# Latent attention with the keys on partitions, 512 queries moving, and the projections made head by head

## What is computed

```python
def mla_queries(c_q, q_norm_g, w_uq, rope):
    q = (rms_norm(c_q, q_norm_g) @ w_uq).reshape(B, L, MLA_HEADS, MLA_QK)
    q_nope, q_rope = q[..., :MLA_NOPE], q[..., MLA_NOPE:]
    if rope is not None:
        q_rope = apply_axial_rope(q_rope, *rope)
    return jnp.concatenate([q_nope, q_rope], axis=-1) * MLA_QK ** -0.5
...
    def one_block(qi):
        s = jnp.einsum('bqhd,bkhd->bhqk', qi, k, preferred_element_type=jnp.float32)
        p = jax.nn.softmax(s, axis=-1).astype(v.dtype)
        return jnp.einsum('bhqk,bkhd->bqhd', p, v)
...
    att = block_softmax_attention(q_lat, jnp.concatenate([k_lat, k_ctx], axis=1),
                                  jnp.concatenate([v_lat, v_ctx], axis=1))
```

## Time and profile before

| | |
|---|---|
| median of 3 runs | 4261.07 us (4256.55 to 4267.57) |
| span of the profiled execution | 4261.7 us |
| attention block, first layer | 440.3 us (503.1 to 943.4) |
| attention block, second layer | 391.8 us (2745.4 to 3137.2) |
| busy over the span: TensorE, VectorE, ScalarE, GpSimd | 87%, 53%, 33%, 31% |
| mean granted TensorE clock | 0.914 |

### The profile page before, as it was taken

How to read it: one execution, slowest core, us unless ns; L and a number is a source line. 1 busy time by engine, 2 the same in 40 slices (tenths; PEclk the granted TensorE clock), 3 DMA queues, 4 the chain that set the end, 5 groups by cost and what they waited for, 6 DMA issues and landing times. The chain is left out here.

```text
span 4261.7 us, 54579 instructions
## 1 busy us (share of the span) xinstructions
PE 3720.1 (87%) x20116; PEld 3116.5 (73%) x20116; DVE 2267.7 (53%) x3970; ACT 1415.5 (33%) x2841; POOL 1306.3 (31%) x1182
## 2 busy tenths in 40 slices
PE   6997688877847899999999897698968788999998
PEld 4897577766625688888888697577847767888886
DVE  4853566656663344444444752576766625445454
ACT  3112466651111422222223312466741123222222
POOL 1211011123331155555554211011123313545454
PEclk8998799997868899999999898799978899999999
DMA  5530000012013111111110630000040122111111
GB/s 188 192 110 3 28 1 13 1 54 112 20 43 141 50 40 39 39 39 39 34 35 10 203 121 4 25 1 11 6 157 20 45 95 69 59 39 52 47 49 54
DMA packets 145678, 243.97 MB, mean 57 GB/s; under 512 B 9480, under 2 KB 113689, under 8 KB 141915
## 3 DMA queue, kind: packets, MB, share of 16 engines
q1 hardware_dynamic: 138108, 208.57, 14.8%
q0 software_dynamic: 7392, 33.03, 2.1%
HBM read 215.60 MB, written 25.99 MB: 57 GB/s over the span
## 5 line engine op out<-in xcount | busy, mean ns | idle before, releaser
L2242 POOL TENSOR_TENSOR x<-x,mlp_tmp 128x512 f32<-128x512 f32 x576 | 785.5, 1396 | 805.9 <-DVE mlp_tmp L2223 800.8
L2223 DVE TENSOR_TENSOR mlp_tmp<-psum,gate 128x512 f32<-128x512 f32 x576 | 391.8, 689 | 273.2 <-POOL x L2242 194.6
L143 PE MATMUL psum<-act_hi,w_hi 128*128 128x512 f32 (+1 forms) x1280 | 472.8, 369 | 12.6 <-DVE w_lo L2201 12.6
L144 PE MATMUL psum<-act_lo,w_hi 128*128 128x512 f32 (+1 forms) x1280 | 472.5, 369 | 0.0
L145 PE MATMUL psum<-act_hi,w_lo 128*128 128x512 f32 (+1 forms) x1280 | 472.4, 369 | 0.0
L143 PE MATMUL psum<-w_hi,hidden_hi 128*128 128x512 f32 x1152 | 449.9, 391 | 0.0
L144 PE MATMUL psum<-w_lo,hidden_hi 128*128 128x512 f32 x1152 | 448.4, 389 | 0.0
L145 PE MATMUL psum<-w_hi,hidden_lo 128*128 128x512 f32 x1152 | 448.2, 389 | 0.0
L2215 DVE TENSOR_TENSOR hidden_lo<-square,hidden_hi 128x512 fp32r<-128x512 f32 x160 | 102.4, 640 | 592.6 <-ACT hidden_hi L2187 592.6
L1378 DVE TENSOR_REDUCE att_max<-psum 128x1 f32<-128x512 f32 (+2 forms) x272 | 217.9, 801 | 183.5 <-PE psum L145 183.3
L2179 ACT ACTIVATE relu<-psum 128x512 f32<-128x512 f32 x160 | 88.9, 555 | 666.8 <-PE psum L145 666.8
(11 more groups left out here) (325 smaller groups left out, 8608.3 us busy)
## 6 DMA issues: line engine op xcount, KB each, us to landing
w_raw<-in_mlp_w SPq DMA_DIRECT2D x128, 512.0 KB, 3.8
side_w<-in_w_ada SPq DMA_DIRECT2D x40, 1024.0 KB, 6.5
hy_tab<-in_hy_tab POOLq DMA_DIRECT2D x24, 1024.0 KB, 13.6
w_raw<-in_w_in SPq DMA_DIRECT2D x32, 512.0 KB, 4.6
ada_w<-in_w_ada SPq DMA_DIRECT2D x8, 1024.0 KB, 11.5
x<-in_x SPq DMA_DIRECT2D x4, 2048.0 KB, 14.6
wo_raw<-in_w_out SPq DMA_DIRECT2D x16, 512.0 KB, 5.6
hy_scratch<-hy_out POOLq DMA_DIRECT2D x24, 256.0 KB, 3.1
```

The costliest lines, as they stand in the source:

```text
L143: pe.matmul(out, lhs[0], rhs[0], start=start, stop=False)
L144: pe.matmul(out, lhs[0], rhs[1], start=False, stop=False)
L2223: dve.tensor_tensor(tmp[:, j % 2, :], ps[:, 4 + j % 4, :], gate[:, int(t >= LAT_TILES), 512 * h:512 * h + 512], ALU.mult).then_inc(gated.s ...
L2242: pool.tensor_tensor(a, a, tmp[:, j % 2, :], ALU.add).then_inc(added.sem, 1)
```

## The change

The attention block is written anew; nothing outside it changes but two tables and the column order of two weights, which are arranged before the launch.

Scores are made with keys on partitions and 512 queries moving (`score`), so the probabilities come out in the layout that the product with the values needs and are not turned. The softmax maximum of a query is then no longer a value per partition. It is found beforehand from a one-pass product of the high parts with queries on partitions (`rough_scores`, a `max_ctx` and four `max_lat` for each block of 512 queries), reduced by VectorE, turned into a row by four transposes (`max_row`), and written with its sign changed by ScalarE into one spare row of the query tile; the key tile holds ones in that row, so the score product itself subtracts it.

The work goes in blocks of one head and 512 queries, and a block in five slots of two key tiles each (in the first layer a block of one slot for each pair of heads holds the context queries). ScalarE takes two exponentials of each slot, one rounded to fp32r into `ph` and one in full precision; VectorE subtracts the two in slots 0, 2 and 4 of a block, GpSimd in slots 1 and 3 (`on_pool`). The value product (`weigh`) runs two slots later in three passes of 512 columns; its weights hold 64 columns of ones beside the 64 values, so it also gives the row sums, which VectorE inverts in two pieces of 64x256 (`invert`) and multiplies in (`normalize`).

Projections are made head by head, channels on partitions, between the slots: the side tasks `q`, `k`, `v` and the maxima of the next block are dealt out over the half slots and share PSUM banks 0 and 1. The rotation of the queries takes two products on VectorE and four instructions on GpSimd for each 512 columns. Both layers' first tasks (`opening`) run before the first slot. At the start of the block GpSimd clears and fills the constant rows, and TensorE and ScalarE wait for it (`fixed`).

```diff
 def latent_first_loads(kit, l, sp):
 
-    QW, KVW = HG * MLA_QK, HG * (MLA_NOPE + MLA_V)
...
+    sp.dma_start(ukv_raw[:], kit.io["mla_w_ukv"][l]).then_inc(kit.sig("lat_ukv_raw", 16).sem, 16)
+    sp.dma_start(uq_raw[:], kit.io["mla_w_uq"][l].rearrange("(t p) n -> p t n", p=P)).then_inc(kit.sig("lat_uq_raw", 16).sem, 16)
+    sp.dma_start(rope[:], kit.io["rope"]).then_inc(rope_in.sem, 16)
+    sp.dma_start(rope_t[:], kit.io["rope_t"]).then_inc(rope_in.sem, 16)
...
+    on_pool = {s for s, (b, j) in enumerate(slots) if j in (1, 3)}
+
+    def max_tasks(b):
+        if blocks[b].context:
+            return [("max_ctx", b, 0), ("row", b, 0)]
+        return [("max_ctx", b, 0)] + [("max_lat", b, i) for i in range(4)] + [("row", b, 0)]
+
+    opening = [("v", 0, g) for g in range(3)] + [("kr", 0, g) for g in range(3)]
+    opening += [("k", 0, g) for g in range(3)] + [("q", 0, g) for g in groups] + max_tasks(0)
+    side = {}
+    for b, block in enumerate(blocks):
+        todo = []
+        if not block.context:
+            todo = [t for n in (b + 1, b + 2) if n < len(blocks) and (n == b + 1 or blocks[n - 1].context) for t in max_tasks(n)]
+            h, p = block.heads[0], block.heads[0] // 2
+            if block.col0 == 0 and h + 1 < MLA_H:
+                todo += [("q", h + 1, g) for g in groups]
+            at = 2 * (h % 2) + (block.col0 > 0)
+            if p + 1 < MLA_H // 2:
+                todo += [("k", p + 1, at)] if at < 3 else []
+                todo += [("v", p + 1, g) for g in {1: [0], 3: [1, 2]}.get(at, [])]
+        n = 2 * block.slots
+        for i in range(n):
+            side[(first[b] + i // 2, i % 2)] = todo[i * len(todo) // n:(i + 1) * len(todo) // n]
...
+            def score(s):
+                b, j = slots[s]
+                if j == 0:
+                    pe.wait_ge(rowed.sem, rowed[b])
+                if s >= 2:
+                    if s - 2 in on_pool:
+                        pe.wait_ge(exped.sem, exped[s - 2])
+                    else:
+                        pe.wait_ge(lo_dve.sem, lo_dve[s - 2])
+                for i in range(2):
+                    k0 = blocks[b].key_tiles[2 * j + i] * P
+                    for h, cols, at in blocks[b].parts():
+                        last = three_pass(pe, ps[:, S0 + 2 * (s % 2) + i, at],
+                                          [a[h // 2 % 2][h % 2][:, k0:k0 + P] for a in (keys_h, keys_l)],
+                                          [a[h % 2][:, cols] for a in (query_h, query_l)], True, True)
...
+            for s in range(n_slots + 2):
+                if s < n_slots:
+                    score(s)
+                    for t in side[(s, 0)]:
+                        side_task(t)
+                if s >= 2:
+                    weigh(s - 2)
+                if s < n_slots:
+                    for t in side[(s, 1)]:
+                        side_task(t)
...
+                scores = ps[:, S0 + 2 * (s % 2):S0 + 2 * (s % 2) + 2, :]
+                act.activation(ph[s % 3][:], scores, ACT.Exp, scale=SCALE)
...
+                    act.activation(scores, scores, ACT.Exp, scale=SCALE).then_inc(exped.sem, 1)
...
+            for b in range(2):
+                for e in range(2):
+                    link(pool, pool.memset(keys_h[b][e][SWAP[e], :].bitcast(F32), 1.0))
+                    link(pool, pool.memset(keys_l[b][e][SWAP[e], :].bitcast(F32), 0.0))
+            for e in range(2):
+                link(pool, pool.memset(query_h[e][SWAP[e], :].bitcast(F32), 0.0))
+                link(pool, pool.memset(query_l[e][SWAP[e], :].bitcast(F32), 0.0))
+            for b in range(2):
+                link(pool, pool.memset(v[b][:, :, V_ONES, :].bitcast(F32), 1.0))
+                link(pool, pool.memset(v[b][:, :, V_ZEROS, :].bitcast(F32), 0.0))
+            pool.memset(kr2[:, :, 32:64], 0.0).then_inc(fixed.sem, 1)
...
+                link(pool, clear)
+                link(pool, pool.tensor_tensor(rot[rows, :], rot[rows, :], rot2[rows, :], ALU.add))
+                link(pool, pool.tensor_copy(query_h[h % 2][rows, cols], rot[rows, :]))
+                pool.tensor_tensor(query_l[h % 2][rows, cols], rot[rows, :], query_h[h % 2][rows, cols].bitcast(F32),
+                                   ALU.subtract).then_inc(roped.sem, 1)
+                pool.wait_ge(roped.sem, roped[t])
...
+            for s in range(n_slots):
+                for t in side[(s, 0)]:
+                    side_task(t)
+                if s in on_pool:
+                    pool.wait_ge(exped.sem, exped[s])
+                    pool.tensor_tensor(pl[s % 3][:], p_sb[:], ph[s % 3][:].bitcast(F32), ALU.subtract).then_inc(lo_pool.sem, 1)
...
+                    if g < 2:
+                        turns = [q for q in tasks[:tasks.index(t)] if q[0] == "q" and q[2] < 2]
+                        if turns:
+                            dve.wait_ge(roped.sem, roped[turns[-1]])
+                        dve.tensor_tensor(rot[ROPE[e], :], bank(t)[ROPE[e], :], rope_t[ROPE[e], cols], ALU.mult)
+                        dve.tensor_tensor(rot2[ROPE[e], :], bank(t)[SWAP[e], :], rope_t[SWAP[e], cols], ALU.mult)
...
+                        link(dve, dve.reciprocal(den[NUM[h % 2], b % 2, c], den[NUM[h % 2], b % 2, c]))
...
+            for s in range(n_slots + 3):
+                if s < n_slots:
+                    for i in range(2):
+                        for t in side[(s, i)]:
+                            side_task(t)
+                    if s not in on_pool:
+                        probs_low(s)
+                if s - 2 in final:
+                    invert(final[s - 2], 0)
+                if s - 3 in final:
+                    invert(final[s - 3], 1)
+                    normalize(final[s - 3])
```

721 lines of the change are left out of this document (371 added, 350 removed).

## The result

The changed kernel took 4411.3 us (4406.7 to 4430.3), the kernel before 4259.1 beside it: ratio 1.0359, 95% interval 1.0336 to 1.0383. The forecast was 4360 in a range of 4215 to 4430, so direction and range held; the likeliest case's own range, 4320 to 4400, ended 11 us short. Of the priced cases the measurement lies between the likeliest, 4363, and the slower clock, 4440, and nearer the second.

A forecast was written before the change was run, and what follows sets the result against it. TensorE's streamed columns bound the attention before; after, its work shrinks but openings, queue stalls and ends add 54.9 us in the second layer and 46.8 in the first: +101.7 on 4261.7 gives 4363, rounded to 4360, range 4215 to 4430.

The forecast's parts named there:

- the likeliest case: Whole kernel: TensorE's work plus opening, queue stalls and end, with nothing absorbed; 4363 us, chance 0.45.
- the slower clock: Rival: TensorE's clock falls in 31 waits of near 3 us, adding 80 us; 4440 us, chance 0.13.
- TensorE's work: Attention by head: 40.8 us after against 45.4 before in the second layer, 43.5 after in the first.
- the sum: Both attention blocks: 446.7 us in the second layer and 487.1 in the first, together +101.7 us.
- The rival by work alone: Queues absorb the stalls and TensorE is the bound throughout; 4219 us, faster, chance 0.20.
- The opening: Start of each layer's attention block to the first slot: 58 us, 58.5 in the first layer, with 11 of TensorE work.
- The gate: Block start: TensorE waits for `fixed` behind 17 GpSimd memsets, so the first product starts 20 us into the block.
- The wait at the row: Before the row transposes TensorE waits for the last maximum: 2.8 us in block (h, 512), 1.1 in (h, 0).
- the rotation: Query rotation: GpSimd's chain takes 4.1 us; one `rot` buffer makes VectorE's second `q` wait, 2.9 us per head.
- The row that the forecast set against this rival: Evidence against the slower clock: before the change, gaps of 1 us left the clock at 0.97.
- The reciprocals: VectorE's 256-column reciprocals, 1.75 us each, four a head (7.0 us), stand in its queue before maxima that TensorE awaits.
- GpSimd beside VectorE: Shared SBUF interfaces: by the skill's rule only the opening's weight subtraction would suffer; no size given.

The follow-up runs named there:

- E5: Changed kernel with constant rows made later, a second pair of rotation buffers and no reciprocals (output not divided by row sums); ratio 0.9946 to the kernel before.
- E1: Changed kernel with GpSimd making rotary keys first and constant rows after, TensorE waiting for the rows only before first reading them; ratio 1.0276 to the kernel before.
- E10: Changed kernel with later constant rows, two rotation buffers, ScalarE's inverse awaited only at the multiply, and eight PSUM banks in the opening; ratio 1.0087 to the kernel before.
- E2: Changed kernel without the two VectorE reciprocals of each block, so the output is not divided by the row sums; ratio 1.0122 to the kernel before.
- E6: Changed kernel with ten unread 512-column products before the wait for the maximum row's bank, in twelve (h, 512) blocks; ratio 1.0317 to the kernel before.
- E8: Changed kernel with later constant rows, two rotation buffers, and reciprocals cut into 128-column pieces spread over four slots; ratio 1.0122 to the kernel before.
- E11: E8 with one reciprocal serving two heads on 128 partitions, the multiply moved to GpSimd, and eight PSUM banks in the opening; ratio 1.0042 to the kernel before.

## Why the prediction was right, and where it fell short

The direction held for the reason given: TensorE's work fell, and an opening and queues that TensorE waits in cost more than was saved. E5 turns the sign by taking three stalls out, though with the division left out. That the time lies within the range is in part owed to the range's width of 215 us: the sum was 51 us low in the blocks, for the clock that it held at full speed, and the rest of the kernel gave back 9.5 us that no term foresaw.

**TensorE's work** was right. The forecast had 315 us in the second layer's slots (326 less 11); E5, at a clock of 0.99, has 312.8 from its first scores on (2790.22 to 3120.33). The rival by work alone, 4219, was a little low even so: E5 measured 4243, without the division and with openings of 48 us (2744.5 to 2792.7) for the 58 assumed.

**The opening** was right in its parts and a little small in sum. The gate was forecast at 20 us and the first product came at 17.8 (520.59 less 502.80); in E1 it came 14.5 us earlier (506.11), and its blocks are 16.3 and 17.1 us shorter. By the windows the openings are 64.7 and 62.8 us for 58.5 and 58. The sum of the forecast also holds 0.15 us for each `max_lat` (2.07, where 0.5, 0.2 and 1.22 make 1.92) that no row shows. The 11 us over are not split here: TensorE works there at a clock of 0.53, which the forecast had for the three `v` alone, and E10's eight banks took 6 us a layer off.

**The queues.** The wait at the row was forecast at 2.8 us in a block (h, 512) and measured at 2.8 to 3.1, and at 1.1 in a block (h, 0), where it was 0.2 on average (22.5 us in 15 waits, 20.7 of them in seven); the rotation at 4.1 for GpSimd and 2.9 for TensorE, measured 4.1 and 2.8 to 3.0 before the product. Idle time of TensorE in the second layer's slots was forecast at 73.7 (388.7 less 315) and was 63.7 (399.90 less 336.21), in the first at 92.6 and was 90.5. These terms stand.

**The term that was mis-sized is the clock**, which the sum held at full speed in the slots and a rival priced at 80 us with a chance of 0.13. By the same windows TensorE was busy 336.2 us for 315 in the second layer and 366.6 for 336 in the first: 21.2 and 30.6, 51.8 us. With 11.0 more in the openings and 12.1 less of idle time in the slots this is the 50.7 by which the two blocks exceeded the forecast. E2, E5 and E6 show that it is the clock: the same instructions are busy 10 us less in E2 and 23 less in E5 in the second layer, 12 and 21 less in the first, and E6, which adds work and takes away idle time alone, is faster. The row that the forecast set against this rival, a clock of 0.97, shows no gap; the trace of that stretch has gaps of mostly 0.7 to 1.3 us, a third of the length of these. Its own price for a gap of 4.65 us, 2.5 us, was the nearer one, and still too high: TensorE has 30 waits of 2.8 us and more in the slots of the two layers, so that 51.8 us are 1.7 for each. That is a mean of unequal ones, nothing behind the 2.81 before 2928.15 and 1.3 behind the 3.07 before 2978.06.

**The rest of the kernel** was taken as unchanged and came out 9.5 us shorter, part before and part behind the second block. One output projection waits 8.61 us where it waited 10.39; the cause of the rest was not looked for.

**The reciprocals** were priced rightly (1.75 us, measured 1742 ns) and their place was not fully tested. The forecast had them late because of their place. E2, without them, wins 91 to 101 us. E8 spread them and won 15 to 24; E11 halved them and, with the banks, won 32 to 34 more, of which the second layer's slots have nothing. In both, a reciprocal still stands ahead of the last maximum, `max_q` is held by GpSimd's subtraction in ten rows, and TensorE waits up to 2.8 us. So the place was not refuted as the cause, and whether VectorE's load, 85% of TensorE's by the forecast, "would fit if it were even" is open: E8 and E11 were not even.

No kernel here that divides by the row sums beats the kernel before: E11 ends 0.4% over it. Two things stay open: an order on VectorE with nothing ahead of the last maximum and `max_q` clear of GpSimd's subtractions, and an inverse that costs VectorE nothing. E5 sets what the second would be worth against E11, about 1%.

**GpSimd beside VectorE.** The prediction expected a conflict over operands in SBUF in the opening's weight subtraction alone. That took 1.22 us, as in the earlier trace rows. `max_q`, which the prediction did not count among the instructions with two operands in SBUF, is where it came: 0.8 us in the changed kernel, 15 to 18 in E8 and E11.

## What to carry to other kernels

Where TensorE waits some 3 us or more for another engine, price the wait as its length plus the slow products behind it, and look for that price in the trace behind several waits of such length, since one can be followed by none. Put what nobody reads for a while (constant rows, buffers to clear) behind the first thing that somebody waits for. An operation whose cost goes by columns should fill all partitions. Less work on an engine shortens a wait only if it goes from ahead of what is waited for: read that engine's queue in the new trace before counting the gain.

## What the runs showed of the hardware that I had not expected

A reciprocal on VectorE costs by columns and next to nothing by partitions: 1742 ns for 64x256, 1753 for 128x256, 943 for 64x128 and 947 for 128x128. From 128 to 256 columns that is 6.2 ns a column; a subtraction goes from 680 ns at 512 to 1222 at 1024, 1.06 a column, so one inverted column is worth nearly six subtracted ones.

VectorE's four-column combination of two operands in SBUF, 0.16 us alone, took up to 2.23 us when it met a GpSimd subtraction of 1024 columns, and ended 0.02 to 0.03 us after it, in every one of the ten cases of E8. VectorE's subtractions, with one operand in PSUM, stayed at 1.2 us beside GpSimd.

A change between ln and exp loaded a table each time, 1283 ns, and the two loads cost more in ScalarE's queue than the 1.2 us of arithmetic.

TensorE's clock came back within 3 us of the work that followed a stall of 3.07 us, and did not fall at all behind one of 2.81. In E11 it fell 1.4 us into the work behind another of 2.81 (the products start 0.23 us apart up to 2882.85 and 0.42 after it). In the openings, where TensorE idles more than half of the time, its mean was 0.53 over more than 60 us.
